# A fp32r transformer pair on one core: the activation buffers of its 512-token stages start 32 bytes later

## What is computed

```python
def swiglu(h, w_in, w_out):                 # w_in [1024, 5632], w_out [2816, 1024]
    g, u = jnp.split(h @ w_in, 2, axis=-1)
    return (jax.nn.silu(g) * u) @ w_out

def ffn_step(s, g, shift, scale, gate, w_in, w_out):
    return s + 0.5 * gate * swiglu(modulate(rms_norm(s, g), shift, scale), w_in, w_out)

# first block: every layer an ffn_step, a mixer, an ffn_step, for x and (until the last mixer) for ctx
# second block: x = x + 0.5 * swiglu_ffn(...); x = x + mixer(...) @ w_out; x = x + 0.5 * swiglu_ffn(...)
```

## Time and profile before

| | |
|---|---|
| time, median of 3 runs | 2894.58 us (2893.55 to 2899.05) |
| profiled execution, first to last instruction | 2891.2 us |
| its own time | not among the three runs; the median is 3.4 us over the span |
| instructions | 49358 |
| TensorE matmul busy | 2770.5 us (96%), 19380 matmuls |
| VectorE busy | 2065.3 us (71%) |
| ScalarE busy | 1025.5 us (35%) |
| GpSimd busy | 81.5 us (3%) |
| mean granted TensorE clock | 0.983 |
| DMA | 421 MB, mean 146 GB/s |

### The profile page before, as it was taken

How to read it: one execution, slowest core, us unless ns; L and a number is a source line. 1 busy time by engine, 2 the same in 40 slices (tenths; PEclk the granted TensorE clock), 3 DMA queues, 4 the chain that set the end, 5 groups by cost and what they waited for, 6 DMA issues and landing times.

```text
span 2891.2 us, 49358 instructions
## 1 busy us (share of the span) xinstructions
PE 2770.5 (96%) x19380; PEld 2447.1 (85%) x19380; DVE 2065.3 (71%) x3075; ACT 1025.5 (35%) x1158; POOL 81.5 (3%) x152
## 2 busy tenths in 40 slices
PE   6999999999999999999999899998999999998999
PEld 4888878888878888788799899887799989986999
DVE  6877778866777777776666766666767766665677
ACT  5222224222232222233344444452144434343433
POOL 1000000000000000000000000000000000000000
PEclk9999999999999999999999999999999999998999
DMA  8444441443334444322245344421044544443354
GB/s 328 160 147 180 172 154 66 161 151 131 131 117 160 146 181 170 112 95 74 84 175 189 131 174 174 180 88 60 3 166 175 202 125 174 185 164 66 117 186 177
DMA packets 68704, 421.42 MB, mean 146 GB/s; under 512 B 7672, under 2 KB 8824, under 8 KB 26592
## 3 DMA queue, kind: packets, MB, share of 16 engines
q1 hardware_dynamic: 48032, 341.26, 31.8%
q0 software_dynamic: 20576, 78.78, 8.4%
HBM read 418.94 MB, written 1.07 MB: 145 GB/s over the span
## 4 chain that ended last, share of the span: by engine, by line
PE 87%; DVE 7%; issue 3%; ACT 2%; DMA 1%; DVEq 0%; SPq 0%; ACTq 0%
PE ps_o L2133 11%; PE ps_o L2135 11%; PE ps_o L2134 11%; PE ps_g L2133 7%; PE ps_u L2133 7%; PE ps_u L2135 7%; PE ps_u L2134 7%; PE ps_g L2134 7%; PE ps_g L2135 7%; PE ps_g L2148 2%; DVE wlo L1191 1%; PE ps_o L2353 1%; ACT whi L706 1%; DMA wraw<-in_W 1%; DVE tsq L1244 1%
## 5 line engine op out<-in xcount | busy, mean ns | idle before, releaser
L706 ACT ACTIVATE whi<-wraw 128x2048 fp32r<-128x2048 f32 x323 | 616.1, 1911 | 788.0 <-PE ps_u L2135 382.8
L1191 DVE TENSOR_TENSOR wlo<-wraw,whi 128x2048 fp32r<-128x2048 f32 x323 | 731.3, 2286 | 160.5 <-ACT whi L706 160.3
L2133 PE MATMUL ps_o<-ah,wlo 128*128 128x256 f32 (+1 forms) x1408 | 462.6, 329 | 19.2 <-issue 15.4
L2133 PE MATMUL ps_g<-hh,wlo 128*128 128x256 f32 (+1 forms) x1464 | 463.3, 316 | 13.2 <-ACT tsq L821 7.4
L2133 PE MATMUL ps_u<-hh,wlo 128*128 128x256 f32 (+1 forms) x1464 | 462.0, 316 | 0.3 <-DVE wlo L1191 0.2
L2135 PE MATMUL ps_g<-hh,whi 128*128 128x256 f32 (+1 forms) x1464 | 462.1, 316 | 0.0
L2135 PE MATMUL ps_u<-hh,whi 128*128 128x256 f32 (+1 forms) x1464 | 462.0, 316 | 0.0
L2134 PE MATMUL ps_u<-hl,whi 128*128 128x256 f32 (+1 forms) x1464 | 461.8, 315 | 0.0
L2134 PE MATMUL ps_g<-hl,whi 128*128 128x256 f32 (+1 forms) x1464 | 461.8, 315 | 0.0
L2135 PE MATMUL ps_o<-ah,whi 128*128 128x256 f32 (+1 forms) x1408 | 454.0, 322 | 0.0
L2134 PE MATMUL ps_o<-al,whi 128*128 128x256 f32 (+1 forms) x1408 | 453.3, 322 | 0.0
(11 more groups left out here) (456 smaller groups left out, 3712.8 us busy)
## 6 DMA issues: line engine op xcount, KB each, us to landing
wraw<-in_W SPq DMA_DIRECT2D x324, 1024.0 KB, 4.8
scr<-in_ADA POOLq DMA_DIRECT2D x126, 512.0 KB, 3.8
scr<-bias_rows POOLq DMA_DIRECT2D x8, 384.0 KB, 8.5
x<-in_XT POOLq DMA_DIRECT2D x1, 2048.0 KB, 10.5
x<-in_MEMT POOLq DMA_DIRECT2D x2, 1024.0 KB, 6.1
cst<-in_CST POOLq DMA_DIRECT2D x1, 1511.5 KB, 7.0
cst<-in_CB POOLq DMA_DIRECT2D x1, 1024.0 KB, 6.6
scr<-in_PM POOLq DMA_DIRECT2D x1, 1024.0 KB, 5.0
```

The source lines that it names most:

```text
L706: nc.scalar.activation(whi[:, n % SLOTS, :], wraw[:, n % SLOTS, :], ACT.Copy).then_inc(w_hi, 1)
L1191: tt_(wlo[:, n % SLOTS, :], wraw[:, n % SLOTS, :], whi[:, n % SLOTS, :].bitcast(f32), sub).then_inc(w_lo, 1)
L2133: mm(out, a[1], b[0], start=first, stop=False)
```

## The change

The two tuples become one, the shifted set. All stages then read and write `hh2`, `hl2`, `ah2` and `al2`; the unshifted set is still declared, takes no memory of its own, and is used by nothing. Addresses in the 256-token layers stay as they are. No instruction is added, left out or moved on any engine, and no wait changes.

```diff
@@ -308,7 +308,8 @@
         with nc.sbuf_tensor("off_a", [128, SHIFT], f32), nc.sbuf_tensor("ah2", [128, 2, NTOK], f32r) as ah2, nc.sbuf_tensor("al2", [128, 2, NTOK], f32r) as al2:
             pass
         hid = sb("hid", [128, 4 * NTOK + 64])
-        wide, narrow = (hh, hl, ah, al), (hh2, hl2, ah2, al2)
+        wide = narrow = (hh2, hl2, ah2, al2)
+        hh, hl, ah, al = wide
         scr = sb("scr", [128, 10240])
```

## The result

The changed kernel takes 2914.69 us (median of 5 runs, 2910.55 to 2917.75); the kernel before, on the same chip, takes 2894.58 us (5 runs, 2892.75 to 2899.05). The ratio is 1.0066, 95% interval 1.0055 to 1.0076: slower by 20 us. The forecast was 2908.6, range 2874 to 2917.

The account below looks back on a forecast made before the run. TensorE's cost per matmul was taken to bound the kernel: +17.6 us for 512-column matmuls and -3.6 for 256-column ones give +14.0, span 2905.2, plus 3.4 to the median: 2908.6 us, range 2874 to 2917.

Parts of the forecast that it names:

- Sign and place: Whole kernel: slower (chance 0.51), with the loss in the 512-token stages and feed-forwards 3 to 7 unchanged.
- The term of the 512 columns: 512-token stages: 4400 matmuls go from 226.7 to 230.7 ns, +4.0 each, +17.6 us in all.
- upper bound: 512-token stages: two shifted 256-column matmuls in place of one of 512, 233.3 ns, +6.7 each, +29.3 us.
- The 256-column passes: 512-token stages: 1047 matmuls go from 120.0 to 117.1 ns, -3.0 us; -3.6 with 384 stationary-activation ones.
- Out of step: Matmul streams: a shift breaks a kept pace, costing 3 to 5 ns more at either size; chance 0.51.
- Reading one: All matmuls: the shift frees 3.3 ns of collision with the weight load at any size; 2875.6 us, chance 0.27.
- Finds a step of its own: 512-column streams keep 226.7 ns when shifted, only 256-column ones win; 2891.0 us, chance 0.22 including no effect.
- 100 ns of room: 512-column streams: weight loads were said to have this much slack within the kept 226.7 ns pace.
- the change does nothing: Whole kernel: no effect at all, 2894.6 us, counted within the same-time case of chance 0.22.

Follow-up runs that it names:

- bare streams: Kernel before plus streams of 48 matmuls with unused results behind its last feed-forward, operand starts varied; 512 columns: 226.7 ns at distance 0, 233.3 at 8.
- ladder of widths: Same added streams on the kernel before, with 4, 32, 64, 96 or 128 stationary columns; 256 columns at distance 0: 119.8 ns with 128, 113.6 with 64.
- half-shifted kernel: Kernel before with only `hh` and `hl` of the 512-token stages shifted, `ah` and `al` not; 2910.42 us, ratio 1.0051.
- SHIFT = 48: Kernel before with the 256-token layers' buffers shifted 48 columns in place of 8, 512-token stages unshifted; 2877.91 us, ratio 0.9935.

## Why the prediction was right

**Sign and place held.** Nearly all of the loss is in the 512-token stages, 23.3 of 24.9 us before feed-forward 3 begins. The wait before feed-forward 3, VectorE's `hl` (478 against 479 ns) and the paces of feed-forwards 3 to 6 stayed. That all loops of 3 to 7 would keep their counts did not hold: feed-forward 7 went from 116.7 to 117.7 ns, 1.5 us that no term has. It is one of the two paces of distance 8 in place of the other; whether the change has any part in that wasn't found. The bare streams show the price of the 512 columns with hardly any transfer under way.

**The term of the 512 columns was mis-sized.** The prediction took +4.0 ns, "since shifted 256-column streams are 3.3 to 4.4 ns over the 113.3 of the stream in step", and had 2 x 116.6 = 233.3 as its upper bound. The streams measured 233.3 (+6.6 ns), the bound itself, and the loop of feed-forward 0 held 1364 matmuls in 318 us in place of the 1380 forecast. With 6.6 ns the sum is 4400 x 6.6 = +29.0 in place of +17.6. The step that failed is the comparison of the two sizes by nearness to a row: 256 shifted columns were taken to have an extra that does not grow with the columns, and the row that was right, two of them in place of one of 512, was used as a bound only. That agreement may be chance: at distance 16 twice 117.8 is 235.6, and 512 columns cost 228.9. At distance 8 itself 256 columns hold 117.8 as well as 116.7.

**The 256-column passes** went to 117.3 by the count, against 117.1 forecast; by their starts they hold 116.6 in feed-forward 0 and 117.8 in 1 and 2, both of the paces of distance 8. There are 181 matmuls in 21 us as forecast, and weight loads take 188 ns:

```profile
L2134 PEld LDWEIGHTS ps_g<-hh,wlo 128*128 128x128 f32 x30 | 5.7, 188 | 0.0
```

**Why the total was nearer than the term.** With the measured price the sum is +29.0 - 3.6 = +25.4 us, and the spans differ by 24.9. This too is nearer than it should be, since 1.5 of the 24.9 are those of feed-forward 7; the stages that the sum is about gave 23.3. Against the medians it is 5 us too much, since the forecast added the 3.4 us by which the profiled execution of before lay under its median, and that of after lay over its own. Part of why 2908.6 came within 6 us of 2914.7 is this, and not the price.

**The mechanism was half right.** "Out of step" said that shifted starts vary, which they do, and that the stretched weight load (192 ns) is why level 256-column matmuls cost 120. The ladder of widths supports that at distance 64 (113.3 with 64 stationary columns or fewer, 120.0 with 128), but not as a rule: at distance 48 it runs the other way, 113.3 with 128 and 118.9 with 64. It also said that a shifted stream has left a kept pace for an irregular one. That is refuted. The shifted stream averages 233.3 as steadily as the unshifted one does 226.7, each distance has its own pace (or two of them, in the 256-token loops), and the half-shifted kernel goes from one to the other as the operand changes. Nor is every shift alike: a 512-column matmul costs 6.6 ns more at 8 columns, 2.4 at 16 in the loop and none at 64. That 512 shifted columns would be slower came out right, by a reason that the runs do not bear out; in that much the forecast was lucky.

**The rivals.** Reading one (3.3 ns less at any size) is refuted at 512 columns, 233.3 against its 223.4. "Finds a step of its own" is refuted for this distance as to time, but its idea stands: with 48 columns of distance 256-column streams hold 113.3 ns with a weight load of 128 columns, which the prediction thought the weight load might forbid. Its "100 ns of room" has no row behind it: a load of 188 ns in a step of 226.7 leaves 39. That the change does nothing is refuted by the interval.

**Two read ports, and the gap of one matmul.** Two independent read ports of TensorE that wait for no one (the Trainium skill, "SBUF — State Buffer", section "SBUF: two separate sides") would leave the distance between two operands without effect. The runs disagree: it moves a 512-column matmul by 6.7 ns and a 256-column one by as much. The N/2.4 + 2.5 ns that the Trainium skill gives for an isolated matmul ("TensorE: Matmul & The Clock Gate", section "Back-to-back issue gap") is 215.8 and 109.2; no stream of fp32r here, each matmul with a weight load of its own, settled under 226.7 and 113.3.

**Open.** What repeats after 256 bytes wasn't seen, only that it does. Why streams at 52 and 60 differ from those at -12 and -4, why a narrow stationary operand makes 512 columns slower at distance 64, and what decides between two kept paces in the 256-token loops is open too; a cause of the weight load's length alone is excluded at 512 columns. Nor does the trace account for the whole gain of `SHIFT = 48`: by the starts its five 256-token loops are 8 us shorter than those of before, its span is 6 us shorter (2885.3 against 2891.2), and the medians are 16 us apart.

## What to carry to other kernels

When a matmul-bound kernel runs some nanoseconds over its columns, measure the pace of bare streams against the distance between the moving and the stationary operand, over one period (here 256 bytes), for each shape that matters, before choosing where buffers begin. A gain at one shape says nothing of another: the 8 columns that win 3.3 ns at 256 columns lose 6.7 at 512. Choose per stage, and check in the kernel, in more than one execution, since a loop can hold another pace than the stream did: bare streams promised 33 us for `SHIFT = 48`, and the kernel kept 16. And count every filler in whole periods, or the control of an experiment isn't one.

## What the runs showed of the hardware that was not expected

- The pace of fp32r matmuls at the upper clock depends on the distance between the starts of their two operands in a partition: 226.7 to 235.6 ns at 512 columns, 113.3 to 120.8 at 256, in streams that wait for nothing. Over distances that are multiples of 32 bytes it repeats after 256 bytes.
- At 512 columns and distance 64 a narrow stationary operand is the slower one: 231.7 ns with 4 or 32 columns, 230.0 with 64 or 96, 226.7 with 128. At 256 columns and distance 48 it can be too: 118.9 ns with 64, 113.3 with 128.
- A stream of the same matmuls on the same bytes can hold one of two paces through a whole loop: 113.3 or 117.7 ns at distance 48, 116.7 or 117.7 at 8, 118.7 or 120.0 at 32. Feed-forward 7 changed from the one to the other between two traces without a change of code or address.
